# Sums of squares in parts and an early table of roots in the head; the first pair's rows copied back behind the next high part

## What is computed

```python
def rms_norm(x, g):
    x32 = x.astype(jnp.float32)
    y = x32 * lax.rsqrt(jnp.mean(x32 * x32, axis=-1, keepdims=True) + RMS_EPS)
    return (y * g.astype(jnp.float32)).astype(x.dtype)

xn = rms_norm(x, attn_norm)
z = xn @ w_in                        # q, k, v, lru_x, lru_gate, merge_gates
...
x = x + (g_a * (o @ w_attn_out) + g_b * ((h * gelu(yg)) @ w_lru_out)) @ w_o
gate, up = split(rms_norm(x, ffn_norm) @ w_gate_up)
x = x + (silu(gate) * up) @ w_down
```

## Time and profile before

| what | value |
|---|---|
| median of 3 runs | 1644.11 us (1642.67 to 1645.88) |
| the profiled execution | 1644.76 us |
| its span, first to last instruction | 1643.0 us |
| TensorE busy | 1607.5 us, 98% |
| VectorE busy | 1027.6 us, 63% |
| GpSimd busy | 997.6 us, 61% |
| ScalarE busy | 644.0 us, 39% |

### The profile page before, as it was taken

How to read it: one execution, slowest core, us unless ns; L and a number is a source line. 1 busy time by engine, 2 the same in 40 slices (tenths; PEclk the granted TensorE clock), 3 DMA queues, 4 the chain that set the end, 5 groups by cost and what they waited for, 6 DMA issues and landing times. The chain is left out here.

```text
span 1643.0 us, 28698 instructions
## 1 busy us (share of the span) xinstructions
PE 1607.5 (98%) x11338; PEld 1540.7 (94%) x11338; DVE 1027.6 (63%) x1717; ACT 644.0 (39%) x1322; POOL 997.6 (61%) x714
## 2 busy tenths in 40 slices
PE   7999999999999999999999999999999999999998
PEld 4999999989999898899899989999999999998998
DVE  7677556865646556768798895333333335868695
ACT  5535552354444535424334443333333334333231
POOL 4645543434425251497868529777777778786876
PEclk9999999999999999999999999999999999999999
DMA  5111123213122131373443312222242222373634
GB/s 193 39 52 65 64 72 99 80 66 114 66 97 66 53 114 49 130 291 123 165 149 132 131 39 103 80 78 79 79 184 79 79 79 79 139 271 130 233 142 152
DMA packets 73033, 182.10 MB, mean 111 GB/s; under 512 B 15092, under 2 KB 26676, under 8 KB 72260
## 3 DMA queue, kind: packets, MB, share of 16 engines
q1 hardware_dynamic: 52228, 160.35, 27.7%
q10 hardware_dynamic: 20672, 19.93, 3.8%
HBM read 131.23 MB, written 49.28 MB: 110 GB/s over the span
## 5 line engine op out<-in xcount | busy, mean ns | idle before, releaser
L642 PE MATMUL bank<-xh,wsh 128*128 128x264 f32 x2170 | 620.1, 286 | 8.4 <-DVE spare L1862 3.8
L642 PE MATMUL bank<-xh,wsl 128*128 128x264 f32 x2170 | 616.8, 284 | 0.0
L642 PE MATMUL bank<-xl,wsh 128*128 128x264 f32 x2170 | 616.0, 284 | 0.0
L642 PEld LDWEIGHTS bank<-xh,wsh 128*128 128x128 f32 x2170 | 408.3, 188 | 11.3 <-issue 8.0
L642 PEld LDWEIGHTS bank<-xl,wsh 128*128 128x128 f32 x2170 | 408.4, 188 | 0.2
L642 PEld LDWEIGHTS bank<-xh,wsl 128*128 128x128 f32 x2170 | 408.4, 188 | 0.0
L642 PE MATMUL bank<-acth,wh 128*128 128x352 f32 x960 | 319.3, 333 | 5.6 <-POOL wl L546 4.1
L642 PE MATMUL bank<-acth,wl 128*128 128x352 f32 x960 | 314.7, 328 | 0.0
L642 PE MATMUL bank<-actl,wh 128*128 128x352 f32 x960 | 314.3, 327 | 0.0
L618 POOL TENSOR_TENSOR wsl<-praw,wsh 128x512 fp32r<-128x512 f32 (+1 forms) x157 | 247.6, 1577 | 70.6 <-ACT wsh L1284 70.4
L544 POOL TENSOR_SCALAR wh<-wraw 128x512 fp32r<-128x512 f32 (+1 forms) x100 | 70.9, 709 | 311.9 <-PE bank L642 292.9
(11 more groups left out here) (187 smaller groups left out, 2428.1 us busy)
## 6 DMA issues: line engine op xcount, KB each, us to landing
praw<-in_weights SPq DMA_DIRECT2D x34, 1024.0 KB, 5.0
wraw<-in_weights SPq DMA_DIRECT2D x52, 512.0 KB, 3.3
h_scratch<-ev SPq DMA_DIRECT2D x44, 264.0 KB, 2.1
acc<-h_scratch SPq DMA_DIRECT2D x4, 2112.0 KB, 12.6
ev<-x_scratch SPq DMA_DIRECT2D x6, 1056.0 KB, 5.0
spare<-x_scratch SPq DMA_DIRECT2D x6, 1056.0 KB, 4.9
praw<-in_weights SPq DMA_DIRECT2D x8, 768.0 KB, 5.3
ta_scratch<-tg ACTq DMA_DIRECT2D x24, 176.0 KB, 1.9
```

The source lines that it names most:

```text
L642: return nc.tensor.matmul(*args, **kw)
```

## The change

It has five parts.

1. TensorE: `raw_block(0, 2)` stands ahead of `sumsq(1)`.
2. ScalarE: a root of eight ones is taken right behind the first block's squares, so that the table is loaded there.
3. ScalarE: the first four high parts of block 0 stand ahead of the second root.
4. VectorE: the sum of block 1 is written out in parts. The first half's first add stands ahead of the first inversion, the rest behind it, and the first four normalizations behind that. The sum of block 2 stands between the two halves of block 0's normalizations, and the second inversion behind them.
5. ScalarE, in ATTN_OUT and OUT: the copy back stands behind the work of r = 1 instead of that of r = 0.

```diff
@@ TensorE, lru_front @@
                     raw_block(0, 0)
                     sumsq(0)
                     raw_block(0, 1)
+                    raw_block(0, 2)
                     sumsq(1)
-                    raw_block(0, 2)
                     raw_block(1, 0)
@@ ScalarE, head @@
             squares(0)
+            f(qstd[:, 0, 0:KC], ones[:, 0:KC], ACT.Sqrt)
             squares(1)
             root(0)
             squares(2)
             rstd_row(0)
+            high(0, range(0, 4))
             root(1)
-            high(0, range(KC))
+            high(0, range(4, KC))
             rstd_row(1)
@@ ScalarE, loop over pairs @@
-                    if r == 0 and p - 1 in (X_FIRST[ATTN_OUT], X_FIRST[OUT]):
+                    if r == 1 and p - 1 in (X_FIRST[ATTN_OUT], X_FIRST[OUT]):
                         copy_back(p - 1)
@@ VectorE, head @@
-            chunk_sum(1, 0, KC, 2)
+            q = xsq[:, 1, :, :]
+            dve.wait_ge(xsq_done, 3)
+            vec(V.tensor_tensor(q[:, 0:2, :], q[:, 0:2, :], q[:, 2:4, :], ALU.add))
             rstd(0)
+            dve.wait_ge(xsq_done, 4)
+            vec(V.tensor_tensor(q[:, 4:6, :], q[:, 4:6, :], q[:, 6:8, :], ALU.add))
+            vec(V.tensor_tensor(q[:, 0:2, :], q[:, 0:2, :], q[:, 4:6, :], ALU.add))
+            V.tensor_tensor(xsum[:, 2, :], q[:, 0, :], q[:, 1, :], ALU.add).then_inc(xchunk_done, 1)
             norm(0, range(0, 4))
+            chunk_sum(2, 0, KC, 3)
+            norm(0, range(4, KC))
             rstd(1)
-            norm(0, range(4, KC))
-            chunk_sum(2, 0, KC, 3)
             norm(1, range(0, 4))
```

## The result

| | before | changed |
|---|---|---|
| median, 20 runs of each in turn | 1644.67 us (1638.85 to 1646.62) | 1646.94 us (1642.20 to 1649.22) |
| ratio | | 1.0016, 95% interval 1.0009 to 1.0023 |
| the profiled execution, its span | 1644.76, 1643.0 us | 1648.40, 1646.6 us |

A forecast was written before the change was run, and what follows sets the result against it. TensorE, busy 98% of the span, bounds the kernel. Head -0.35, ATTN_OUT 0 and OUT 0 took the profiled 1644.76 to 1644.4 us, or 1643.8 us against the median of 1644.11; range 1641.4 to 1646.9 us.

The forecast's parts named there:

- everything behind the copy, put at nothing: Rest of the kernel after the copy in OUT: the sum, -0.35 + 0 + 0, has no term for it.
- Head, ScalarE: Head: early table and small root fit ScalarE's wait and cost nothing; first root at 17.1 instead of 18.37 us.
- Head, VectorE: Head: VectorE's adds and GpSimd's steps take turns; normalization starts at 23.1 us, last low part ends 0.35 us earlier.
- rival (c): Head: the turns are dealt badly, 1.45 us slower, 1645.6 us; chance 0.11.
- the forecast of -0.35: Head's net term: GpSimd's last low part ends at 52.45 instead of 52.80 us, 0.35 us gained.
- Head, TensorE: Head: the 2.34 us wait for the third sum goes; the stop for the last low part grows from 1.01 to 3.0 us.
- ATTN_OUT: Second pair of ATTN_OUT: the 2.14 us stop goes, the later wait grows from 0.34 to 2.5 us; gain 0.
- The bound of 0.6 us: ATTN_OUT: possible loss of 0.6 us if the next weights get between the pieces of the gates' load.
- Rival (a), the clock: Behind a longer stop, in the head or at 802.7 us, clock falls to 0.50, costing 1.4 or 2.9 us; chance 0.27.
- OUT: Second pair of OUT: ScalarE's copy ends later, but TensorE has no stop from 877 to 935 us; cost nothing.

The follow-up runs named there:

- table_order: Kernel before with only the early table of roots and TensorE's raw_block(0, 2) ahead of sumsq(1); ratio 1.0016 (1.0005 to 1.0028).
- looks 1 and 4: Two of four further single profiled executions of the changed kernel, nothing altered; 1647.75 us (look 1) and 1644.91 us (look 4).
- copy_only: Kernel before with only the copy back moved behind r = 1 in ATTN_OUT and OUT; ratio 1.0001 (0.9991 to 1.0010).
- head_only: Changed kernel with the copy back at r == 0 as before, so the head's four parts alone; ratio to the kernel before 1.0013 (1.0002 to 1.0024).
- sum2_tensor: Kernel before with two of block 2's three adds taken off VectorE, TensorE adding four rows instead; ratio 0.9996 (0.9987 to 1.0004).
- sum1_whole: head_only with block 1 summed whole ahead of the first inversion; ratio to the kernel before 0.9995 (0.9983 to 1.0006).
- head_filled: head_only with two unused products by ones inside TensorE's last stop of the head; ratio to the kernel before 1.0010 (0.9999 to 1.0022).
- two_waits: Kernel before with two more satisfied waits at the start of VectorE's list; ratio 1.0002 (0.9993 to 1.0011).
- head_again: head_only unchanged, run a second time beside head_filled; ratio to the kernel before 1.0017 (1.0005 to 1.0030).
- gpsimd_later: head_only with GpSimd's four weight steps of unit 0 behind the eight low parts of block 0; one execution, 1649.06 us.

## Why the prediction was wrong, point by point

Two steps failed: the turns in the head, taken as fixed, and everything behind the copy, put at nothing. The copy's own term was mis-sized, without a cost in time that shows.

- **Head, ScalarE:** right about the table; and worth nothing by itself (`table_order`: first normalization at 23.16 us). What it put at nothing was the root's next wait, for TensorE's first sum: 0 to 0.54 us in nine executions.
- **Head, VectorE: the step of the sum that failed.** I wrote down one order of turns ("19.85 to 20.7, 21.5 to 22.3 and 22.7 to 23.2") as if it were fixed. It is what five of nine executions do (first normalization at 23.2 to 23.7 us); in the other four GpSimd is first, and it stands at 24.4 to 24.8 us. This is rival (c), which priced the bad order at 1.8 us over the other; the two kinds lie about 1.1 us apart. Its chance was 0.11 and should have been near a half. The add was due at 19.85 us, and GpSimd's step stands at 20.21 us in the trace of before: 0.4 us apart, when the root alone waited up to 0.54 us for TensorE. Where the add was first, the forecast of -0.35 us came true (-0.48 and -0.33 us in looks 1 and 4); where GpSimd was, the head lost 0.35 to 1.02 us. What the row of 5.91 us said of block 2's adds held (5.92 again).
- **Head, TensorE:** the 2.34 us wait for the sum went, but up to 0.96 us of another wait on the same product took its place, and 0.95 us stand before the first split product. The third stop is 1.7 to 1.8 us instead of 3.0, since the other two took their part; the end is set by GpSimd either way.
- **ATTN_OUT:** the mechanism was right, the term was mis-sized: the later stop is 2.7 us where I had 2.5, and 3.9 in the executions in which a fetch of instructions falls into the load. The bound of 0.6 us was for the wrong cause. With `copy_only` at 1.0001 the gain of 0 stands.
- **Rival (a), the clock:** a fall stood behind the longer stop in all nine executions that have the new place of the copy and the load in one piece, twice for 6.8 us. But behind the old stop of 2.1 us, at 1.00 in the one trace that I had, falls of 3.4 us followed in `head_only`, `table_order`, `sum2_tensor`, `sum1_whole`, `head_filled` and `two_waits` too, and not in two others. So most of what (a) charges was being paid already. From 780 to 860 us TensorE lost 0.60 us against the trace of before in `two_waits`, which has the old copy, and 0.72, 0.88, -0.04, 0.68 and 0.76 in the five.
- **OUT:** right, no stop near the copy.
- **Everything behind the copy, put at nothing:** the largest term that I can name. The sum ends with the copy, but from 1500 to 1536 us, around the stop at 1533 us, the five executions lost 1.25, 2.78, 0.05, 1.20 and 0.09 us against the trace of before, 1.1 in the mean; the 2.78 holds a fall of the clock.

Where the five lie against the one trace of before, by TensorE's products and in the mean: they end 2.8 us later (3.65, 2.99, 3.15, 3.94 and 0.16). Of that, 0.6 us is there at 20 us already (0.26 to 0.88), since the clock came to full speed at 13.8 to 14.5 instead of 12.8 us. To 55 us, counted from the raw product at 20 us, they lost 0.59, -0.48, 1.02, 0.35 and -0.33 us, 0.2 in the mean where I had -0.35. From 55 to 780 us it is 0.3 us, where falls of the clock differ in number and length; at ATTN_OUT 0.6 us, as in `two_waits` with the old copy; at 1533 us 1.1 us. So the head's turns and the stop at 1533 us make 1.3 us that belong to the change, 1.65 above the forecast of -0.35. That the first 0.6 us is chance is likely and not shown: `copy_only` has 0.75 there at a ratio of 1.0001, `head_again` -1.02 at 1.0017. What makes the rest of the 2.6 us between the medians stays open.

The median lies 0.04 us outside the range. Inside it, it would have been luck: the range held one outcome of each race, not their sum, and nothing of the stop at 1533 us.

## What to carry to other kernels

Where two engines take turns at memory, look at when each arrives: a row shows one dealing of the turns. If they arrive within a few tenths of a microsecond of each other, both orders are outcomes with a chance of their own, and an edit that moves work out of a stretch in which the other engine is idle (VectorE's whole sum here, from 17.09 us, when GpSimd's first step comes at 19.38) into one where it is busy buys a gamble. When a wait is taken away, ask what the same step waits for next, and how much that moves from run to run: the table had kept 1.6 us between TensorE's first sum and the root, and with them TensorE's slow start didn't matter. Take work away from the pair instead (one add for three brought the first product of block 2 forward by 0.9 us), and split a transfer so that what is needed first comes first. In a kernel at 98% of its bound, look through the whole trace for pairs that nearly collide: a list that is two entries longer shifted one of them here.

## What was unexpected of the hardware

- A fetch of 16 KB of TensorE's instructions (0.96 us on one DMA engine) inside a load of 1056 KB made it 6.1 to 6.3 us instead of 4.9 to 5.0, and moved with the length of TensorE's list alone.
- VectorE paused for 0.46 us instead of 0.10 at one place of its list, and whether it does depends on what stands ahead; the pause at 1522 us decided a race with GpSimd worth 1.2 us.
- The same kernel showed falls of the granted clock of 3.4 us behind stops of 1.8 to 2.1 us in some executions and not in others; behind those of 2.7 to 4.2 us near 806 us and in the head of `gpsimd_later` in every one profiled.
- In 20 traces TensorE's first 4 to 10 raw products stood 0.59 us apart before the distance fell to 0.30 us. In the changed kernel this start, 2.8 to 6.1 us long, goes together with whose turn it was between VectorE and GpSimd.
